# A gated delta rule in a two-block kernel: chunks worked in pairs, and a version with three chunks interleaved

## The chip, the cores and the metric

The kernel runs on one core of a Trainium2 chip, all in fp32. The metric is the time of one execution on the device in microseconds; lower is better. It is a long program of many stages (projections, scans, two attentions, a delta rule, merges), and each stage ends with a barrier of all engines. The change touches one stage, the delta rule, and two tables of constants that it reads.

## What is computed

The stage is the gated delta rule of the second block, run forwards and backwards over 1280 tokens (256 of context, then 1024), for 8 heads of 64 channels, in chunks of 64 tokens, so 20 chunks:

```python
gc = cumsum(g)                                       # per chunk
decay = exp(gc_i - gc_j), lower triangle
lower = strict_lower((k*beta) @ k.T * decay);  A = lower + I
u, w  = solve(A, v*beta), solve(A, k*beta*exp(gc))
qk    = (q @ k.T) * decay
# then, chunk after chunk
v_new = u - w @ S
o     = (q*exp(gc)) @ S + qk @ v_new
S     = S*exp(gc_last) + (k*exp(gc_last-gc)).T @ v_new
```

All but the last three lines is independent from chunk to chunk (the solve). The last three lines carry the state S from chunk to chunk (the advance).

## The kernel before, in words

The class is `Delta` (L1819 to L2166). Partitions 0 to 63 hold the forward chunk and partitions 64 to 127 the backward one, so one chunk step works on 2 directions x 8 heads. The inverse of A is built by doubling: a start from the 2x2 blocks, then `ROUNDS` = 5 rounds. In each round, `ym = -(ct_i x xm)`, then `xm += xt x ym` and `xt += ym x xt`, where `ct_i` is the lower triangle masked to the level of the round. The five masked copies are made by GpSimd (L1916), from `lt`.

TensorE works on 64x64 tiles of its array. `product` (L1932), `to_channels` (L1942) and `with_state` (L1950) each issue 16 small matmuls, one for each head and direction, and `tile_position` says on which quarter of the array each runs. With `src` and `dst` equal (both 0 or both 1) only the two diagonal quarters are used, otherwise all four are. Each fp32 matmul of 64x64 appears in the trace as two weight loads and two matmuls, so that one product is 32 + 32 records.

The order of work is written out by hand. `pairs` (L1870) takes chunks two by two: `weave` alternates the steps of `solve(c)` and `solve(c+1)` on every engine, then `advance(c)` and `advance(c+1)` follow one after the other, and then the next pair starts. Every engine runs its instructions in the order in which they are issued; the engines wait for each other on semaphores. Two sets of buffers and the 8 PSUM banks (4 for each chunk) limit the work to two chunks.

The steps of one chunk in the kernel before:

- SP loads q, k and v (L1889) and the gates beta and g (L1890, L1891), two DMAs of each, before each chunk.
- VectorE spreads the gates (L2055 to L2057) and makes k*beta (L2058). TensorE sums the gates (L1964 to L1967, one product of 512 columns and three narrow ones), and ScalarE takes the exponentials (L2128 to L2131). VectorE scales the queries (`qg`, L2061).
- TensorE transposes k, k*beta, q and qg (L1973, 16 transposes). ScalarE and VectorE copy them out (L2134, L2135, L2064).
- TensorE makes the scores (L1980), VectorE masks and decays them (L2069 to L2072), TensorE turns the first level (L1987, L1992), VectorE starts the inverse (L2077, L2079).
- Five rounds: TensorE (L1938), ScalarE takes `ym` out of PSUM (L2144), TensorE two products, VectorE adds them (L2087, L2090); the last round ends with L2011, L2012 and ScalarE's L2148.
- TensorE makes u and w, ScalarE and VectorE copy them (L2151, L2095).
- The advance: products with the state (L1953), `vn` (L2104), the state's decay (L2109), two more products (L1946, L1938), the state (L2111), the output (L2161, L2114), and two stores on ScalarE's DMA queue (L2164, L2165).

Of the kernel before, what the change touches and what calls it, by code (L numbers as in the profile page):

```python
# [14 lines left out]
P = 128  # L15
# [13 lines left out]
CTX = 256  # L29
# [1789 lines left out]
class Delta(Stage):  # L1819


    N = T2 // 64
    HALVES = (slice(0, 64), slice(64, P))
    ROUNDS = 5

    def __init__(self, k, dn, dg, o_dn):
        super().__init__(k, "delta")
        self.dn, self.dg, self.o_dn = dn, dg, o_dn
        t, sig, N = self.tile, self.event, self.N
        self.ones, self.sums, self.tri, self.sm = t("ones", [P, P]), t("sums", [P, 3, P]), t("tri", [P, 8, 64]), t("sm", [P, 2, 256])  # L1830
        two = lambda name, *shape: [t(f"{name}{s}", [P, *shape]) for s in range(2)]
        self.x, self.gb, self.gm, self.gd, self.dec, self.ex, self.gt = two("x", 1536), two("gb", 16), two("gm", 512), two("gd", 16), two("dec", 512), two("ex", 16), two("gt", 8)
        self.kb, self.vb, self.kbg, self.qg, self.kd = two("kb", 512), two("vb", 512), two("kbg", 512), two("qg", 512), two("kd", 512)
        self.tq, self.tk, self.lt, self.qk, self.ct = two("tq", 4, 3, P), two("tk", 4, P), two("lt", 512), two("qk", 512), two("ct", 6, 512)
        self.xm, self.xt, self.ym, self.um, self.wt, self.vn, self.o = two("xm", 512), two("xt", 512), two("ym", 512), two("um", 512), two("wt", 2, 256), two("vn", 512), two("o", 512)
        self.consts, self.cleared = sig("dma", "consts", 2), sig("dve", "cleared", 1)
        self.loaded = [sig("dma", f"loaded{s}", 6 * N // 2) for s in range(2)]
        self.stored = [sig("dma", f"stored{s}", 2 * N // 2) for s in range(2)]
        (self.gated, self.scaled_q, self.copied_q, self.lowered, self.ct0, self.qk_ready, self.w_copied, self.v_new, self.state, self.outputs) = (
            sig("dve", x, N) for x in ("gated", "scaled_q", "copied_q", "lowered", "ct0", "qk_ready", "w_copied", "v_new", "state", "outputs"))  # L1840
        self.vbeta, self.dec_masked, self.decayed = (sig("pool", x, N) for x in ("vbeta", "dec_masked", "decayed"))
        self.decays, self.copied_k, self.final, self.u_copied, self.o_copied = (sig("act", x, N) for x in ("decays", "copied_k", "final", "u_copied", "o_copied"))
        (self.summed, self.turned, self.scored, self.flipped, self.moved, self.u_made, self.w_made, self.ws, self.qs, self.grown, self.inner) = (
            sig("pe", x, N) for x in ("summed", "turned", "scored", "flipped", "moved", "u_made", "w_made", "ws", "qs", "grown", "inner"))
        R = self.ROUNDS
        self.xt_ready, self.xm_ready, self.levels = sig("dve", "xt_ready", N * R), sig("dve", "xm_ready", N * R), sig("pool", "levels", N * R)
        self.y_made, self.y_copied = sig("pe", "y_made", N * R), sig("act", "y_copied", N * R)
        self.x_fix, self.xt_fix = sig("pe", "x_fix", N * (R - 1)), sig("pe", "xt_fix", N * R)

# [4 lines left out]
    @staticmethod  # L1854
    def heads(t):
        return t.rearrange("p (h b d) -> p b h d", b=2, h=4)

# [4 lines left out]
    def mask(self, l, rows=slice(0, P)):  # L1862
        return bc(self.tri[rows, l].unsqueeze(1), [rows.stop - rows.start, 8, 64])

    @staticmethod
    def turn(c, i, n):

        return 2 * n * (c // 2) + 2 * i + c % 2

    def pairs(self, solve, advance):  # L1870
        for c in range(0, self.N, 2):
            yield from weave(solve(c), solve(c + 1))
            yield from advance(c)
            yield from advance(c + 1)

    def sp(self):
        SP, N = self.nc.sync, self.N
        SP.dma_start(self.sums[:], self.a["c_sums"]).then_inc(*self.consts.inc())
        SP.dma_start(self.tri[:], self.a["c_tri"]).then_inc(*self.consts.inc())
        for c in range(N):  # L1880
            s = c % 2
            x, gb, loaded = self.x[s], self.gb[s], self.loaded[s]
            if c >= 2:
                SP.wait_ge(*self.scaled_q(c - 2))
                SP.wait_ge(*self.decayed(c - 2))
                SP.wait_ge(*self.turned(c - 2))
            for j, first in enumerate((c * 64, CTX + 64 * (N - 1 - c))):
                rows, tokens = self.HALVES[j], slice(first, first + 64)
                SP.dma_start(x[rows], self.dn[tokens, :]).then_inc(*loaded.inc())  # L1889
                SP.dma_start(gb[rows, 0:8], self.dg[tokens, 8 * j:8 * j + 8]).then_inc(*loaded.inc())  # L1890
                SP.dma_start(gb[rows, 8:16], self.dg[tokens, 16 + 8 * j:24 + 8 * j]).then_inc(*loaded.inc())  # L1891
            yield

    def pool(self):
        self.nc.gpsimd.wait_ge(*self.consts(1))
        yield from self.pairs(self.pool_solve, lambda c: iter(()))

    def pool_solve(self, c):
        G, s, h3 = self.nc.gpsimd, c % 2, self.h3
        k_, v_ = self.x[s][:, 512:1024], self.x[s][:, 1024:1536]  # L1900
        beta, ex = self.gb[s][:, 0:8], self.ex[s]
        G.wait_ge(*self.loaded[s](6 * (c // 2) + 5))
        if c >= 2:
            G.wait_ge(*self.outputs(c - 2))
        G.tensor_tensor(h3(self.vb[s][:]), h3(v_), self.per(beta), ALU.mult).then_inc(*self.vbeta.inc())
        yield
        G.wait_ge(*self.decays(c))
        G.tensor_tensor(h3(self.dec[s][:]), h3(self.dec[s][:]), self.mask(0), ALU.mult).then_inc(*self.dec_masked.inc())
        G.wait_ge(*self.gated(c))
        G.tensor_tensor(h3(self.kd[s][:]), h3(k_), self.per(ex[:, 8:16]), ALU.mult)  # L1910
        G.tensor_tensor(h3(self.kbg[s][:]), h3(self.kb[s][:]), self.per(ex[:, 0:8]), ALU.mult).then_inc(*self.decayed.inc())
        yield
        yield
        G.wait_ge(*self.lowered(c))
        for l in range(2, 7):
            G.tensor_tensor(h3(self.ct[s][:, l - 1]), h3(self.lt[s][:]), self.mask(l), ALU.mult).then_inc(*self.levels.inc())  # L1916
        yield

    def pe(self):
        PE = self.nc.tensor  # L1920
        PE.wait_ge(*self.consts(1))
        PE.wait_ge(*self.cleared(0))
        yield from self.pairs(self.pe_solve, self.pe_advance)

    def places(self):

        for j in range(4):
            for par in range(2):
                for r in range(2):
                    yield r, par, j, slice(64 * (2 * j + par), 64 * (2 * j + par) + 64)  # L1930

    def product(self, bank, left, right, src=0, dst=0):  # L1932


        for r, par, j, cols in self.places():
            i, o = r ^ (src & par), r ^ (dst & par)
            rows = self.HALVES[i]
# [544 lines left out]
```

## Time and profile before

| what | value |
|---|---|
| runs of the kernel before | 5002.05 us median of 3 (4998.92 to 5014.29) |
| the profiled execution | 5008.63 us |
| its span in the trace | 5006.8 us |
| TensorE, VectorE, ScalarE, GpSimd busy, whole program | 69%, 47%, 25%, 19% |
| instructions, whole program | 74740, of these 31808 matmuls and 31808 weight loads |

A line of the profile's list of groups gives source line, engine, operation, output and inputs, shapes and count, then busy time and mean duration, then the idle time of the engine just ahead of it and what ended it ("issue" is idle time that nothing in the profile explains). A line of the timeline begins with the start and the duration in us. A group of matmuls in it ends when the last result is out of the array, and the next group can start before that, so the pace of products is read from start to start.

### The profile page before, as it was taken

To read this page: it belongs to the slowest core of one execution; us is meant where nothing else is said; L and a number is where in the kernel's file an instruction comes from. 1 tells how busy PE (TensorE), PEld (TensorE's weight loads), DVE (VectorE), ACT (ScalarE), POOL (GpSimd) and SP (SyncE) were. 2 spreads that over 40 slices of the span, in tenths; PEclk is the share of its full clock that TensorE was granted. 3 is DMA by queue.
4 is the path that set the end of the run, shared out by engine and by line. 5 is a ranking of instruction groups with operands and counts; after the bars stand their busy time and mean duration, and the time that the engine had idled before them with its cause. 6 is when DMAs were issued, how large, how long until landed. Compare 5 with 4: busy or idle time off the path is not lost. (4 is left out here: it accounts for less than half of the span.)

```text
span 5006.8 us, 74740 instructions
## 1 busy us (share of the span) xinstructions
PE 3460.5 (69%) x31808; PEld 2829.7 (57%) x31808; DVE 2352.9 (47%) x3815; ACT 1237.1 (25%) x2052; POOL 951.9 (19%) x761
## 2 busy tenths in 40 slices
PE   4997554664879955547493998971566577777588
PEld 4996443243379954435343997960455466666233
DVE  2113885474621158857564101115578645545333
ACT  2112330243321123314332111101243322222232
POOL 1211332010011123310011112201111133333100
PEclk9997666897989965569795999985677689889789
DMA  3231003432323210031223212213322111110421
GB/s 121 95 101 47 20 20 106 124 82 93 114 91 103 81 41 20 14 112 34 84 98 112 76 63 98 99 62 129 144 96 81 53 27 35 37 35 22 168 82 44
DMA packets 244971, 383.33 MB, mean 77 GB/s; under 512 B 48223, under 2 KB 188439, under 8 KB 243228
## 3 DMA queue, kind: packets, MB, share of 16 engines
q1 hardware_dynamic: 146218, 253.10, 15.8%
q10 hardware_dynamic: 98422, 125.45, 7.3%
q8 instruction: 252, 4.13, 0.3%
q14 instruction: 79, 0.65, 0.0%
HBM read 261.61 MB, written 123.03 MB: 77 GB/s over the span
## 5 line engine op out<-in xcount | busy, mean ns | idle before, releaser
L350 PE MATMUL psum<-proj_w_low,h_high 128*128 128x344 f32 (+1 forms) x2016 | 664.9, 330 | 54.6 <-POOL proj_w_low L334 54.6
L350 PE MATMUL psum<-proj_w_high,h_high 128*128 128x344 f32 (+1 forms) x2016 | 663.2, 329 | 0.0
L350 PE MATMUL psum<-proj_w_high,h_low 128*128 128x344 f32 (+1 forms) x2016 | 663.0, 329 | 0.0
L369 DVE COPY proj_y<-psum 128x344 f32<-128x344 f32 (+1 forms) x126 | 67.8, 538 | 921.7 <-PE psum L350 921.7
L350 PEld LDWEIGHTS psum<-proj_w_low,h_high 128*128 128x128 f32 x2016 | 380.7, 189 | 59.2 <-issue 55.7
L350 PEld LDWEIGHTS psum<-proj_w_high,h_low 128*128 128x128 f32 x2016 | 380.4, 189 | 3.9
L350 PEld LDWEIGHTS psum<-proj_w_high,h_high 128*128 128x128 f32 x2016 | 380.4, 189 | 3.7
L334 POOL TENSOR_TENSOR proj_w_low<-proj_raw,proj_cut 128x2752 fp32r<-128x2752 f32 (+1 forms) x30 | 193.1, 6437 | 976.8 <-DVE proj_cut L363 976.8
L393 ACT ACTIVATE proj_y<-psum 128x344 f32<-128x344 f32 (+1 forms) x126 | 59.2, 470 | 732.8 <-PE psum L350 732.8
L1247 PE MATMUL psum<-merge_wo,merge_yt 128*128 128x512 f32 x512 | 226.7, 601 | 13.4 <-ACT merge_yt L1192 10.0
L950 PE MATMUL psum<-diff_kk,diff_q 64*128 64x512 f32 x512 | 136.3, 653 | 104.8 <-ACT diff_w L1033 71.5
L350 PE MATMUL psum<-proj_latents_w_low,h_high 128*128 128x448 f32 x512 | 189.6, 370 | 20.1 <-POOL proj_latents_w_low L334 20.1
L1033 ACT ACTIVATE diff_w<-psum,diff_nm 128x1024 f32<-128x1024 f32 x128 | 142.5, 1114 | 242.0 <-DVE diff_nm L1003 233.7
L525 PE MATMUL psum<-scan_mqs,scan_mks 64*128 64x128 f32 (+1 forms) x2048 | 162.6, 383 | 46.8 <-DVE scan_am L651 42.8
L350 PE MATMUL psum<-roj_latents_w_high,h_high 128*128 128x448 f32 x512 | 189.3, 370 | 0.0
L350 PE MATMUL psum<-roj_latents_w_high,h_low 128*128 128x448 f32 x512 | 189.3, 370 | 0.0
L1527 PE MATMUL psum<-na_kk,na_q 64*128 64x512 f32 (+2 forms) x320 | 90.4, 719 | 142.3 <-DMA na_v<-proj 102.8
L525 PEld LDWEIGHTS psum<-scan_mqs,scan_mks 64*128 64x128 f32 (+1 forms) x2048 | 144.3, 280 | 66.9 <-issue 58.1
L1247 PEld LDWEIGHTS psum<-merge_wo,merge_yt 128*128 128x128 f32 x512 | 97.3, 193 | 133.8 <-issue 116.7
L651 DVE COPY_PREDICATED scan_am<-scan_lmask,psum 128x512 f32<-128x512 uint32 x224 | 162.5, 725 | 16.5 <-PE psum L525 10.8
L1002 DVE TENSOR_REDUCE diff_nm<-psum 128x1 f32<-128x1024 f32 x128 | 156.3, 1221 | 20.6 <-PE psum L950 20.3
L369 DVE COPY proj_latents_y<-psum 128x448 f32<-128x448 f32 x32 | 20.0, 625 | 295.1 <-PE psum L350 295.1
(418 smaller groups left out, 7300.9 us busy)
## 6 DMA issues: line engine op xcount, KB each, us to landing
proj_raw<-in_w_in SPq DMA_DIRECT2D x24, 1376.0 KB, 6.8
proj<-proj_y ACTq DMA_DIRECT2D x192, 172.0 KB, 1.9
dn_prep_x<-proj SPq DMA_DIRECT2D x24, 768.0 KB, 7.0
delta_x<-dn_qkv SPq DMA_DIRECT2D x40, 384.0 KB, 4.1
proj_latents_raw<-in_w_in SPq DMA_DIRECT2D x8, 1792.0 KB, 7.7
proj<-proj_latents_y ACTq DMA_DIRECT2D x64, 224.0 KB, 1.9
proj<-proj_y ACTq DMA_DIRECT2D x60, 216.0 KB, 1.9
norm_x<-x_stream SPq DMA_DIRECT2D x24, 512.0 KB, 3.2
```

What stands on the lines that cost most here:

```text
L334: G.tensor_tensor(self.wl[:, c % 2], self.raw[:], self.cut[:], ALU.subtract).then_inc(*self.low.inc())
L350: last = PE.matmul(self.ps[:, j % 4, 0:self.width], hp[:, kt, tokens], wp[:, c % 2, kt, :], start=kt == 0 and n == 0, stop=kt == KT - 1 an ...
L369: V.tensor_copy(self.y[:, j % 4, :], self.ps[:, j % 4, 0:self.width]).then_inc(*self.copied[1].inc())
L393: S.activation(self.y[:, j % 4, :], self.ps[:, j % 4, 0:self.width], ACT.Copy).then_inc(*self.copied[0].inc())
L525: last = PE.matmul(out, mk[rows, l, tile, :], mq[rows, l, tile, :], start=True, stop=True, tile_position=(rows.start, 0))
L651: placed = V.copy_predicated(dst, mask.bitcast(U32), sc)
L950: last = PE.matmul(ps[:, 2 * cc + half, :], self.q[rows, s, t * P:(t + 1) * P], self.kk[rows, s, half * 512:(half + 1) * 512], start=True, ...
L1002: c(V.reduce_max(nm[:, z, cc:cc + 1], self.both(cc), axis=AX))
L1033: S.activation(self.w[:, z, cc], self.both(cc), ACT.Exp, bias=self.nm[:, z, cc:cc + 1], scale=0.125, accum_out=self.sm[:, z, cc:cc + 1]).t ...
L1247: last = PE.matmul(ps[:, 4 * s + 2 + half], self.yt[:, s, j * P:(j + 1) * P], self.wo[:, j, half * 512:(half + 1) * 512], start=j == 0, st ...
L1527: last = PE.matmul(ps[:, 2 * h + b, at:at + width], self.q[rows, g, t * P:(t + 1) * P], self.kk[rows, g, c0:c0 + width], start=True, stop= ...
```

## The change

The stage `Delta` is rewritten.

- Three sets of buffers (`SETS = 3`), two PSUM banks for each set and two shared banks for the advance. The order is no longer `pairs` and `weave`: every step of a chunk has a due time written at its `yield` (0 for the first, 20.75 for the last), chunk c starts at 6c (`PACE = 6`), and every engine issues steps in the order of due times, the older chunk first where they are equal. The advance of chunk c-3 (18 to 20.75) so falls among the first steps of chunk c (0 to 2.75).
- The backward direction is mirrored on arrival: two products of TensorE with a reversing matrix, 64 rows by 512 columns each, turn k and v of partitions 64 to 127, and ScalarE writes them back (due 0 and 0.25). The masks are the same for both directions then.
- All gates are loaded once ahead of the first chunk, with four DMAs for each chunk, 80 in all, and TensorE waits for all of them. The loads of q, k, v stay, two DMAs for each chunk.
- A round: the first product uses `lt` itself, not a masked copy; VectorE masks and negates on the way out of PSUM, and only the half of the columns that the level needs; the second product (all four quarters) is as before; the third keeps its two quarters but has 32 moving columns for each matmul, not 64; VectorE adds half of the columns in each of the two sums. ScalarE has no part in the rounds. GpSimd's masked copies are gone.
- The queries are not scaled before the transposes. The product of q and the state is scaled by VectorE when it is copied out. 12 transposes, not 16. `wt` is copied by ScalarE, and `decay` of the state is made by GpSimd, into a second buffer.
- One more narrow product in the gate sums; the mask of the scores with the queries is two VectorE operations of 64 partitions.

The diff, cut to what the text speaks of:

```diff
+    SETS = 3
+    PACE = 6
-    def pairs(self, solve, advance):
-        for c in range(0, self.N, 2):
-            yield from weave(solve(c), solve(c + 1))
-            yield from advance(c)
-            yield from advance(c + 1)
+    def chunks(self, program):
+        return by_time(*(paced(program(c), self.PACE * c, 1) for c in range(self.N)))
...
     def sp(self):
...
+            for rows, t, first in ((self.HALVES[0], at, 0), (self.HALVES[1], back, 8)):
+                SP.dma_start(self.gates[rows, c, 0:8], t[:, first:first + 8]).then_inc(*self.gated_in.inc())
+                SP.dma_start(self.gates[rows, c, 8:16], t[:, 16 + first:24 + first]).then_inc(*self.gated_in.inc())
+        yield from self.chunks(self.sp_chunk)
...
     def pe(self):
+        self.nc.tensor.wait_ge(*self.gated_in(4 * self.N - 1))
...
+        yield 0
+        self.mm(ps[H[1], B, :], 1, 1, self.tri[H[1], 8], x[H[1], 512:1024])
+        self.mm(ps[H[1], B + 1, :], 1, 1, self.tri[H[1], 8], x[H[1], 1024:1536]).then_inc(*self.mirrored.inc())
+        yield 1
...
+            yield 6 + 2 * i
+            for r, par, j in self.places():
+                rows, o = H[r], r ^ par
+                last = self.mm(at(o, col(B + par, 0, j, 64)), r, o, grp(self.lt[s])(rows, par, j), grp(xm)(rows, par, j))
+            last.then_inc(*self.y_made[i].inc())
+            yield 7 + 2 * i
+            PE.wait_ge(*self.y_copied[i](c))
+            if i < R - 1:
+                for r, par, j in self.places():
+                    h, rows = r ^ par, H[r ^ par]
+                    self.mm(at(r, col(B + par, 0, j, 64)), h, r, grp(xt)(rows, par, j), grp(ym[i])(rows, par, j))
+                for r, par, j in self.places():
+                    h, rows = r ^ par, H[r ^ par]
+                    last = self.mm(packed(at(h, col(B, 256 + 128 * par, j, 32)), i), h, h, grp(ym[i])(rows, par, j), side(grp(xt)(rows, par, j), i, 1))
...
+        yield 18
+        for r, par, j in self.places():
+            self.mm(at(r, col(A + par, 256, j, 64)), par, r, tq[H[par], j, 1, H[r]], sm[H[par], r, 64 * j:64 * j + 64])
+        for r, par, j in self.places():
+            last = self.mm(at(r, col(A + par, 0, j, 64)), par, r, wt[H[par], r, 64 * j:64 * j + 64], sm[H[par], r, 64 * j:64 * j + 64])
+        last.then_inc(*self.ws.inc())
+        yield 19
         PE.wait_ge(*self.v_new(c))
         PE.wait_ge(*self.o_copied(c))
...
     def dve_chunk(self, c):
+        yield 0.5
+        V.wait_ge(*self.placed(c))
         V.tensor_copy(gd[0:64, 0:8], g[0:64])
         V.tensor_copy(gd[64:128, 8:16], g[64:128])
         V.tensor_tensor(h3(self.gm[s][:]), self.mask(0), per(g), ALU.mult)
         V.tensor_tensor(h3(self.kb[s][:]), h3(k_), per(beta), ALU.mult).then_inc(*self.gated.inc())
...
+            yield 6.5 + 2 * i
+            V.wait_ge(*self.y_made[i](c))
+            V.tensor_tensor(sides(self.ym[i][s][:], i, 0), part, minus, ALU.mult).then_inc(*self.y_copied[i].inc())
+            yield 7.5 + 2 * i
+            V.wait_ge(*self.fixed[i](c))
+            V.tensor_tensor(left, left, part, ALU.add)
+            V.tensor_tensor(right, right, ps[:, B, 256:512].rearrange("p (b n u) -> p b n u", b=2, u=2 << i), ALU.add).then_inc(*self.updated[i].inc())
+        yield 18.5
         V.wait_ge(*self.ws(c))
...
+        yield 18.75
+        V.tensor_tensor(o, ps[:, A:A + 2, 256:512].rearrange("p b (h d) -> p b h d", h=4), bc(faded.unsqueeze(3), [P, 2, 4, 64]), ALU.mult).then_inc(*self.o_copied.inc())
```

## Rows read from the trace of the kernel before

**Rows 1.** The page: the span, and the queue that carries instructions (packets, MB, share).

```profile
span 5006.8 us, 74740 instructions
...
q8 instruction: 252, 4.13, 0.3%
```

**Rows 2.** Stretches: engines' busy us (instructions), TensorE clock, DMA share, GB/s.

```profile
3975.40:4642.00 666.60, 467.86 (x15840) 420.74 (x15840) 332.32 (x484) 135.01 (x280) 228.50 (x180) 0.89 0.15 36
...
4247.00:4259.00 12.00, 11.00 (x43) 9.25 (x44) 5.79 (x9) 3.10 (x10) 7.36 (x6) 0.57 0.14 38
...
4268.00:4296.00 28.00, 19.63 (x932) 18.53 (x932) 10.99 (x17) 6.35 (x11) 7.01 (x6) 1.00 0.02 5
```

**Rows 3.** Groups of instructions by line in the stage, two that the change removes.

```profile
L1916 POOL TENSOR_TENSOR delta_ct<-delta_lt,delta_tri 128x512 f32<-128x512 f32 x100 | 133.1, 1367 | 19.8 <-DVE delta_lt L2069 19.8
...
L2144 ACT ACTIVATE delta_ym<-psum 128x512 f32<-128x512 f32 x100 | 57.3, 596 | 269.8 <-PE psum L1938 269.8
```

**Rows 4.** The timeline of TensorE: one advance, then within the rounds of a pair.

```profile
4237.64 0.69 PE L1946 MATMUL psum<-delta_vn,delta_kd 64*64 64x64 f32 x32 [0.81 <-ACT delta_o L2161]
...
4239.05 0.97 PE L1938 MATMUL psum<-delta_vn,delta_qk 64*64 64x64 f32 x27 [0.65 <-issue]
...
4270.72 0.68 PE L1938 MATMUL psum<-delta_ym,delta_xt 64*64 64x64 f32 x32
4271.18 1.07 PE L1938 MATMUL psum<-delta_xt,delta_ym 64*64 64x64 f32 x30
4272.04 0.27 PE L1938 MATMUL psum<-delta_ym,delta_xt 64*64 64x64 f32 x2
...
4274.95 0.51 PE L1938 MATMUL psum<-delta_xm,delta_ct 64*64 64x64 f32 x19 [0.58 <-issue]
...
4278.71 0.85 PE L1938 MATMUL psum<-delta_xt,delta_ym 64*64 64x64 f32 x21 [1.08 <-issue]
...
4282.70 0.86 PE L1938 MATMUL psum<-delta_xt,delta_ym 64*64 64x64 f32 x23 [0.98 <-issue]
```

**Rows 5.** The timeline at the stage's start and end, and an earlier row of small DMAs.

```profile
3975.43 0.33 SPq L1878 DMA_DIRECT2D delta_sums<-in_c_sums  x1
...
3982.57 0.60 SPq L1890 DMA_DIRECT2D delta_gb<-dn_gates  x1
3983.21 0.60 SPq L1891 DMA_DIRECT2D delta_gb<-dn_gates  x1
3983.32 0.16 DVE L2055 COPY delta_gd<-delta_gb 64x8 f32<-64x8 f32 x1 [6.67 <-DMA delta_gb<-dn_gates]
...
4639.43 0.34 SPq L2194 DMA_DIRECT2D merge_nw<-in_dn_norm_w  x1
...
L1349 SPq DMA_DIRECT2D rpb_skewed<-rpb_rows x64: 766/767/915, 949.5 to 1000.8; - x64
```

**Rows 6.** Narrow products at the lower clock, and transposes at the higher one.

```profile
4252.47 0.57 PE L1966 MATMUL psum<-delta_gb,delta_sums 128*128 128x8 f32 x2
4252.90 0.59 PE L1967 MATMUL psum<-delta_gd,delta_ones 128*128 128x16 f32 x2
...
3996.92 0.60 PE L1973 MATMUL psum<-ident,delta_x 128*128 128x128 f32 x4
3997.36 0.60 PE L1973 MATMUL psum<-ident,delta_qg 128*128 128x128 f32 x4
```

**Rows 7.** VectorE operations of 256 and of 512 columns, and one beside GpSimd.

```profile
3962.38 0.42 DVE L1752 TENSOR_TENSOR dn_prep_e<-dn_prep_y,dn_prep_rp 128x256 f32<-128x256 f32 x1
...
4265.79 0.67 DVE L2077 TENSOR_TENSOR delta_xm<-delta_tri,psum 128x512 f32<-128x512 f32 x1
...
4245.88 1.46 DVE L2057 TENSOR_TENSOR delta_gm<-delta_tri,delta_gb 128x512 f32<-128x512 f32 x1
```

**Rows 8.** ScalarE: a DMA issue (the first of two), and its next activation.

```profile
4240.90 0.45 ACTq L2164 DMA_DIRECT2D o_dn<-delta_o  x1
...
4242.52 0.60 ACT L2161 ACTIVATE delta_o<-psum 128x512 f32<-128x512 f32 x1 [5.02 <-issue]
```

More of the change, by code:

```diff
@@ L1837, in __init__ @@
[L1837 to L1841, printed above, removed]
@@ L1894, in pool, with sp_chunk @@
+    def sp_chunk(self, c):
+        SP, Z, s = self.nc.sync, self.SETS, c % self.SETS
+        yield -8
+        if c >= Z:
+            SP.wait_ge(*self.gated(c - Z))
+            SP.wait_ge(*self.decayed(c - Z))
+            SP.wait_ge(*self.turned_q(c - Z))
+        for first, rows in zip((c * 64, self.back(c)), self.HALVES):
+            SP.dma_start(self.x[s][rows], self.dn[first:first + 64]).then_inc(*self.loaded[s].inc())
     def pool(self):
         self.nc.gpsimd.wait_ge(*self.consts(1))
-        yield from self.pairs(self.pool_solve, lambda c: iter(()))
@@ L1925, in places @@
[L1925 to L1937, printed above, removed]
-            last = self.nc.tensor.matmul(self.ps[self.HALVES[o], bank + par, 64 * j:64 * j + 64], left[rows, cols], right[rows, cols], start=True, stop=True,
-                                         tile_position=(64 * i, 64 * o))
-        return last
@@ new lines, in pe, with mm @@
+    def pe(self):
+        self.nc.tensor.wait_ge(*self.consts(1))
+        self.nc.tensor.wait_ge(*self.cleared(0))
+        self.nc.tensor.wait_ge(*self.gated_in(4 * self.N - 1))
+        back = self.HALVES[1]
+        self.mm(self.ps[back, 0, 0:16 * self.N], 1, 1, self.tri[back, 8], self.gates[back].rearrange("p c g -> p (c g)")).then_inc(*self.gates_turned.inc())
+        yield from self.chunks(self.pe_chunk)
+    def mm(self, out, i, o, left, right, start=True, stop=True):
+        return self.nc.tensor.matmul(out, left, right, start=start, stop=stop, tile_position=(64 * i, 64 * o))
@@ L2008, in pe_solve @@
-        for r, par, j, cols in self.places():
-            swapped, rows = self.HALVES[r ^ par], self.HALVES[r]
-            out, at = ps[rows, near + par, 64 * j:64 * j + 64], (64 * (r ^ par), 64 * r)
-            PE.matmul(out, eye[swapped], xt[swapped, cols], start=True, stop=False, tile_position=at)
-            last = PE.matmul(out, ym[swapped, cols], xt[swapped, cols], start=False, stop=True, tile_position=at)
-        last.then_inc(*self.xt_fix.inc())
-        yield
-        PE.wait_ge(*self.final(c))
@@ new lines, in pe_chunk @@
+        last.then_inc(*self.grown.inc())
+        yield 20
+        PE.wait_ge(*self.state(c))
+        for r, par, j in self.places():
+            last = self.mm(at(r, col(A + par, 0, j, 64)), r, r, grp(self.qk[s])(H[r], par, j), grp(self.vn[s])(H[r], par, j))
+        last.then_inc(*self.inner.inc())
+    def dve(self):
+        V = self.nc.vector
+        for s in range(self.SETS):
+            V.memset(self.gd[s][:], 0.0)
+            for ym in self.ym:
+                V.memset(ym[s][:], 0.0)
+        V.memset(self.ones[:], 1.0)
```

432 lines of the change are left out of this document (214 added, 218 removed).

## The prediction

> **What bounds the kernel now.** The change touches one stage, so I first took its length. It begins at 3975.4 and the next stage begins at 4639.4 [rows 5], so it is 664.0 us of the profile's 5006.8 [rows 1]. The stretches come second: in 666.6 us TensorE is busy for 468, VectorE for 332, GpSimd for 229, ScalarE for 135 [rows 2]. No engine is full. With first work at 3983.3, ten pairs take 656 us: 65.6 us each, 32.8 for each chunk. The groups by line come third: GpSimd's masked copies (133 us) and ScalarE's evictions in the rounds (57 us, 270 us of waiting ahead of them) lie beside or between TensorE's products [rows 3].
>
> The timeline of the rounds shows what TensorE waits for. A product on four quarters lets the next one start 0.46 us later, one on two quarters 0.86 us later [rows 4]. But at 4274.95, 4278.71 and 4282.70 TensorE stands for 0.58, 1.08 and 0.98 us on "issue", in the middle of a product, 3.76 and 3.99 us apart. Between two such stops lie about 126 matmuls and as many weight loads. The program has 63,616 of these, and the instruction queue brought 252 packets [rows 1], so about 252 instructions each. I read the stops as the arrival of the next packet of TensorE's instructions: **a packet (126 matmuls) takes at least 3.88 us**, however fast the array is. That is an inference from the regular distance. In 28 us of rounds 932 matmuls, 7.4 packets, pass, and 7.4 x 3.88 = 28.7: the rounds are bound by it, at the full clock of 1.00 [rows 2].
>
> **The change, part by part.** In matmul records of one chunk: before, the stage has 15,840 / 20 = 792 [rows 2]. After: mirror 4, sums 10, transposes 12, scores 32, turning 48, rounds 4 x 96 + 32 + 64, u and w 64, advance 128, in sum 778. TensorE's instructions so stay: 778 / 126 = 6.2 packets, a floor of 24.0 us for each chunk.
>
> Start. 80 gate DMAs stand on SP's queue ahead of the first chunk's load, and TensorE waits for the last. Such a DMA takes 0.64 us of the queue (3982.57 to 3983.21), 51.2 us in all. With the loads behind them and 4 us of landing, the first product starts 57.4 us after the stage's begin, where work now starts after 7.9: **+49.5 us**, with no cover, since the stage stands between barriers. Bounds: 0.33 us each, as the first DMA of the stage, gives +25; 0.81 (64 DMAs in 51.3 us, L1349) gives +63 [rows 5].
>
> Prices in the steady state, at the full clock: a product on four quarters 0.46, on two 0.89; results are out 0.23 us after that, and the next engine starts 0.13 later. Mirroring has 4 records of 512 columns on one quarter; 32 records of 64 columns on two quarters take 0.86, so 0.054 each and 1.7 us for mirroring. Four transposes take 0.44 [rows 6]. VectorE takes 0.67 for 512 columns and 0.42 for 256; two SBUF operands beside GpSimd cost 1.46 [rows 7]. ScalarE takes 0.60, so at most 1.2 for the 1024 columns of the mirrored part (I take 1.1); its two DMA issues hold it for up to 1.6, I take 1.3 [rows 8].
>
> The third product of a round, 32 columns on two quarters, has no row. Columns alone would give 0.46. Weight loads may bind instead: narrow products of 8 columns follow each other at 0.43 for two records at the lower clock, 0.11 a record at the full one for 128 weight columns [rows 6], so 0.05 for 64, and on two quarters 0.8. I take 0.75, the row nearest to it. The Trainium skill ("TensorEngine Tiling (Array Packing)", Instruction Overhead) says that a matmul of one column takes as long as one of 60, and to take no factor from a dimension that is already small; by it the product stays at 0.86. Four-quarter records follow at 0.46 / 32 = 14 ns, so no such floor holds across quarters; within one no row decides. By the rule a period would be 0.2 us longer.
>
> One period (6 units of due time) then goes, by the written order, from the start of the mirroring of chunk c:
>
> - mirror 1.9, handoff, ScalarE 1.1, VectorE's gates beside GpSimd's `vb` 2.4, and **only then** `o` of chunk c-3 (due 18.75, behind the gates at 0.5): 0.6. TensorE's next step, `kd` of c-3, waits for that `o`. With handoffs 6.3 us, 4.6 of them idle on TensorE. Three chunks in work do not cover this, since every later product is queued behind `kd`.
> - `kd` 0.46, two double products 2 x 1.21, sums 1.8, ScalarE 1.2, the last of the products issued meanwhile: 6.3 to the transposes.
> - transposes, ScalarE's two copies, then its DMA issues, `final` and the queries' copy: 5.1 to the scores.
> - scores 1.1, VectorE 2.7, turning 1.1, VectorE 1.4, handoffs, `y0` 0.46: 7.2 to the next mirroring.
>
> In sum 24.9 us without the packets. VectorE's work in it is 14, TensorE's 17, GpSimd's 6: none is the bound. The state's own loop (products, `vn`, `kd`, sum) is 4 us and is never last.
>
> Packets. I walked this order with a packet boundary every 128 records (near the 126 read off) and 3.9 us at least between two, from four positions of the boundary in the period. I take it that the idle 4.6 us can't be saved up: at 4239.05 TensorE stops for 0.65 us though it had waited 0.81 shortly before [rows 4]; the dense parts after it stop for 0.6 to 1.9 us three or four times. The periods are 27.9, 28.2, 29.0 and 30.0 us: **28.7**.
>
> Fill and drain: first three periods 22, 23 and 26 us, the last partial ones 20, 13 and 9: 113 us, in place of 3 full periods.
>
> Stage: 57.4 + 113 + 17 x 28.7 = 658.3 us, against 664.0: 5.7 us less. Against the profiled 5008.6 that is 5002.9. That execution is 6.6 us over the median, so I predict **4996 us**. A us in the period is 17 us in the time; that is where the risk lies. What is removed elsewhere (masked copies, ScalarE in the rounds, 4 transposes) I cost at nothing of its own: it is in the order above, and TensorE's packets are the cover.
>
> **The rivals.** About 0.3% (15 us) is what a measurement of this kernel can tell from no change.
>
> A, faster: the packets are fetched further ahead than I think, and the period comes near the written chain, or part of the chain is shorter. For it: the floor of 24.0 us and the chain's 24.9. Against it: the stop shortly after a wait [rows 4]. With 26 us: 57 + 110 + 442 = 609, 55 us less, 4947.
>
> B, slower: the clock. In 4247 to 4259, after an advance in which TensorE mostly waits, the granted clock is 0.57, near the lower level of 1.2 GHz; in the dense rounds it is 1.00 [rows 2]. The change puts an idle stretch of 4.6 us into every period, ahead of a dense part of 6 us. If each is followed by a lower clock, the dense part takes up to 6 us more, about half hidden by the packets: period 31.5, 57 + 118 + 535 = 710, 46 us more, 5048. It decides from about 1.2 us of period on. In its favour the Trainium skill ("TensorE: Matmul & The Clock Gate", HAM oscillation) describes bursts that start cold after each wait, every time; against it, four-quarter products keep the array fuller than the sums and transposes that ran in the slow stretch.
>
> C, slower: VectorE's half-width operations read runs of 2, 4, 8 columns. If one costs as much as a full one, the chain has four more of 0.3: period 30, 22 us over the forecast: 5018.
>
> **Chances.** The forecast (period 27.7 to 29.7) 0.40; A 0.27; B 0.25; C 0.08. The forecast's own range, 4979 to 5013, reaches from faster (a third) to no difference. So faster 0.40, same 0.24, slower 0.36. Its range reaches halfway past A and B, since the start's bounds (-25 and +14) come on top: 4930 to 5065.
>
> **What would show it.** In the profile after: SP issues for 51 us before TensorE's first product of the stage; mirroring starts 28.7 us apart; `kd` waits for `o` with 4 to 5 us of idle TensorE; "issue" stops of about 1 us, 3.9 us apart, in the dense parts; instruction packets unchanged; VectorE's round operations at 0.42; the third product 0.75 from start to start. Wrong would be: gate DMAs far from 0.64 us, products denser than 126 matmuls in 3.9 us, or a granted clock under 0.8 in the steady state (B).

## The result, and the profile after

The change makes the kernel **slower**: 5089.36 us (median of four, 5074.09 to 5102.16) against 5008.17 for the kernel before in the same session. The ratio is 1.0162 [1.0127, 1.0197], so 81 us more. I had forecast 4996, with a range up to 5065.

The profiled execution is the slowest of the four, 5102.16 us. Its page, beside [rows 1], with the busy times:

```profile
span 5100.4 us, 73846 instructions
...
PE 3546.6 (70%) x31530; PEld 2890.3 (57%) x31530; DVE 2313.0 (45%) x3916; ACT 1213.9 (24%) x2013; POOL 829.6 (16%) x681
...
q8 instruction: 249, 4.08, 0.3%
```

The work is what the prediction counted: 278 matmuls fewer (14 for each chunk, less 2 that turn the gates once at the start) and three instruction packets fewer. The engines do less, and still the span is 93.6 us longer.

The stage's own marks say where. First SP's queue and TensorE at the start, then the first and last mirroring copy, and the first DMA of the next stage (timeline, then single lines with minimum, median and maximum duration in ns and the first and last start):

```profile
3973.28 0.33 SPq L1922 DMA_DIRECT2D delta_sums<-in_c_sums  x1
...
L1927 SPq DMA_DIRECT2D delta_gates<-dn_gates x40: 474/596/605, 3974.1 to 4023.9; - x40
...
4031.28 3.67 PE L1984 MATMUL psum<-delta_x,delta_tri 64*64 64x512 f32 x4 [3.42 <-DMA delta_x<-dn_qkv]
...
L2186 ACT ACTIVATE delta_x<-psum x20: 1018/1018/1019, 4035.0 to 4662.5; 64x1024 f32<-64x1024 f32 x20
...
L2248 SPq DMA_DIRECT2D merge_nw<-in_dn_norm_w x1: 336/336/336, 4732.8 to 4732.8; - x1
```

The stage takes 4732.8 - 3973.3 = 759.5 us, where it took 664.0. It divides into five parts:

| part | predicted | measured |
|---|---|---|
| start to the first mirroring | 57.4 | 58.0 |
| first mirroring to its copy | not counted | 3.7 |
| first three intervals between mirroring copies | 22, 23, 26 | 26.3, 25.8, 29.4 |
| the next sixteen | 28.7 each | 34.1 each |
| from the last copy to the end | 70.7 | 70.3 |

The start and the end are as worked out. The stage is 101 us longer than the 658.3 forecast: sixteen periods of 5.4 us too much are 87 of them, the first three intervals 10.5, the first mirroring 3.7. So the question is mostly what lies in a period. Stretches of the kernel after (columns as in [rows 2]): the first interval between mirroring copies, the last of the rounds, the mirroring and the idle stretch in three pieces, the dense part after it, the steady state as a whole, and two single periods out of it:

```profile
4035.00:4061.30 26.30, 15.20 (x155) 10.32 (x158) 6.84 (x12) 3.77 (x9) 4.31 (x4) 0.50 0.19 45
...
4300.00:4317.00 17.00, 15.21 (x594) 14.33 (x592) 8.12 (x17) 3.85 (x7) 4.27 (x4) 0.86 0.26 65
...
4317.00:4321.00 4.00, 1.91 (x17) 0.44 (x6) 1.71 (x5) 1.02 (x1) 0.95 (x1) 1.00 0.02 6
4321.00:4322.00 1.00, 0.00 (x0) 0.00 (x0) 0.99 (x3) 0.00 (x0) 0.09 (x1) 0.89 0.00 0
4322.00:4323.00 1.00, 0.00 (x0) 0.00 (x0) 1.00 (x2) 0.00 (x0) 0.00 (x0) 0.50 0.00 0
...
4323.00:4336.00 13.00, 12.83 (x266) 11.66 (x267) 3.21 (x8) 1.07 (x5) 1.91 (x2) 0.52 0.01 3
...
4152.00:4662.00 510.00, 406.70 (x11671) 356.26 (x11670) 210.91 (x420) 83.44 (x180) 79.71 (x75) 0.78 0.13 31
...
4255.90:4285.30 29.40, 22.29 (x778) 19.63 (x778) 13.85 (x28) 5.54 (x12) 5.33 (x5) 0.94 0.16 39
4489.90:4526.60 36.70, 29.21 (x779) 25.74 (x778) 14.02 (x28) 5.56 (x12) 5.31 (x5) 0.72 0.13 31
```

The granted clock is 1.00 through the mirroring and the first part of the idle stretch, falls shortly before 4322 while TensorE still stands, is 0.50 (the lower level of 1.2 GHz) in the last us of it, and 0.52 in the 13 us after it. The mean of the steady state is 0.78; the kernel before had 0.89 in its stage [rows 2]. By 0.78, some 15 of the 34.1 us of a period run at the lower level (an estimate from these two numbers). The periods differ, and with the clock: with the same 778 or 779 matmuls and about the same wait of `kd`, the one at 0.94 took 29.4 us, near the 28.7 of the forecast, the one at 0.72 took 36.7. Here is the period with the idle stretch above in the timeline:

```profile
4317.03 1.88 PE L1984 MATMUL psum<-delta_x,delta_tri 64*64 64x512 f32 x4
...
4318.95 1.02 ACT L2186 ACTIVATE delta_x<-psum 64x1024 f32<-64x1024 f32 x1 [7.60 <-PE psum L1984]
...
4320.05 1.04 POOL L1957 TENSOR_TENSOR delta_vb<-delta_x,delta_gates 128x512 f32<-128x512 f32 x1 [15.32 <-ACT delta_x L2186]
4320.18 0.94 DVE L2116 COPY delta_gd<-delta_gates 64x8 f32<-64x8 f32 x1
...
4321.74 0.68 DVE L2118 TENSOR_TENSOR delta_kb<-delta_x,delta_gates 128x512 f32<-128x512 f32 x1
4322.34 0.68 DVE L2161 TENSOR_TENSOR delta_o<-psum,delta_ex 128x512 f32<-128x512 f32 x1
4323.17 1.13 PE L1984 MATMUL psum<-delta_vn,delta_kd 64*64 64x64 f32 x32 [4.25 <-DVE delta_o L2161]
4324.05 1.10 PE L1984 MATMUL psum<-delta_ym,delta_xt 64*64 64x64 f32 x32
...
4327.46 1.91 PE L1984 MATMUL psum<-delta_xt,delta_ym 64*64 64x32 f32 x32
...
4329.30 2.07 PE L2003 MATMUL psum<-delta_gm,delta_sums 128*128 128x512 f32 x2
```

`kd` (L1984 in this line: one helper issues all small products) starts 6.14 us after the mirroring and waits 4.25 us for VectorE's `o`, which stands behind the gates of the new chunk. That is the wait that I had forecast, 6.3 and 4.6. What follows is slow: the next product starts 0.88 us after `kd`, where four quarters took 0.46 at the full clock [rows 4]. VectorE's half-width operations are not dear; here is the group that makes `ym`, all rounds, from 4136 to 4663:

```profile
L2144 DVE TENSOR_TENSOR delta_ym<-psum,delta_minus 128x256 f32<-128x256 f32 x78 | 31.9, 422 | 31.0 <-PE psum L1984 28.7
```

### The profile page after: what moved, and what is told of

Its sections match the earlier page's. It is cut to its first block and busy times, and to the rows that moved or that the text cites. A ratio compares the mean times of both kernels' runs of the same rounds, so it can differ in the third digit from the quotient of the medians.

```text
span 5100.4 us, 73846 instructions
## 1 busy us (share of the span) xinstructions
PE 3546.6 (70%) x31530; PEld 2890.3 (57%) x31530; DVE 2313.0 (45%) x3916; ACT 1213.9 (24%) x2013; POOL 829.6 (16%) x681
```

## The experiments

Nine kernels. E1, E2, E6 and E8 change the kernel after in one place; E3, E5 and E7 put E1 and E2 together, E3 and E7 with one more edit; E10 changes the kernel before; E4 is a small kernel by itself. Ratios are to the kernel before on the same chip, with the 95% interval. A ratio below 1 is faster. Periods and clocks are those of the one profiled execution of each kernel, and this is not always the median one: it was 13 us above the median for the kernel after (5102.16), 24 us below it for E2 (4934.54) and 9 us below it for E8 (5015.17), so differences of periods between these come out somewhat too large.

### E1: the gates in 4 DMAs instead of 80

```diff
-        for c in range(N):
-            at, back = self.dg[c * 64:c * 64 + 64], self.dg[self.back(c):self.back(c) + 64]
-            for rows, t, first in ((self.HALVES[0], at, 0), (self.HALVES[1], back, 8)):
-                SP.dma_start(self.gates[rows, c, 0:8], t[:, first:first + 8]).then_inc(*self.gated_in.inc())
-                SP.dma_start(self.gates[rows, c, 8:16], t[:, 16 + first:24 + first]).then_inc(*self.gated_in.inc())
+        ahead = self.dg[0:64 * N].rearrange("(c p) g -> p c g", p=64)
+        back = self.dg[CTX:CTX + 64 * N].rearrange("(c p) g -> p c g", p=64)[:, ::-1]
+        for rows, t, first in ((self.HALVES[0], ahead, 0), (self.HALVES[1], back, 8)):
+            SP.dma_start(self.gates[rows, :, 0:8], t[:, :, first:first + 8]).then_inc(*self.gated_in.inc())
+            SP.dma_start(self.gates[rows, :, 8:16], t[:, :, 16 + first:24 + first]).then_inc(*self.gated_in.inc())
```

> Edit: the 80 gate DMAs of the changed kernel become 4, one for each direction and each of beta and g, with all 20 chunks in each; nothing else. Theory (the start is a plain sum: 80 DMAs of 0.64 us on SP's queue with no cover): the first mirroring moves from 58 us after the stage's begin to 10 to 14 us, and the time falls by 44 to 48 us, from 5089 to about 5043. Rival (descriptors, not issues, are the cost: the 4 DMAs move 5120 pieces of 32 bytes): the first mirroring comes 30 us or more after the begin and the gain is under 30 us. In both the period stays 33 to 34 us.

Measured: 5035.61 us, ratio 1.0075 [1.0053, 1.0096], 0.9% less than the kernel after. One of the two lines of gate DMAs (2 of the 4), and TensorE's first mirroring:

```profile
L1927 SPq DMA_DIRECT2D delta_gates<-dn_gates x2: 663/716/768, 3981.6 to 3984.0; - x2
...
3992.86 3.67 PE L1984 MATMUL psum<-delta_x,delta_tri 64*64 64x512 f32 x4 [1.71 <-DMA delta_x<-dn_qkv]
```

The stage began at 3980.8, so mirroring starts 12.1 us after the begin instead of 58.0. That is 45.9 us less in one place, and by the ratios 0.87%, some 43 us, in the time. The period stays at 33.8 us and the clock at 0.78. The start costs what was predicted and has nothing to do with the miss.

### E2: `o` of the old chunk ahead of the gates of the new one

```diff
     def dve_chunk(self, c):
...
-        yield 0.5
+        yield 0.8
         V.wait_ge(*self.placed(c))
```

The old chunk's `o` is due at 18.75, so 0.75 in the new chunk's count; the gates now come behind it.

> Edit: in the changed kernel VectorE's gates of chunk c get the due time 0.8 in place of 0.5, so the output o of chunk c-3 (0.75) goes ahead of them and the product kd no longer waits for the mirroring, ScalarE's copy and the gates; nothing else. Theory 1 (the idle 4.25 us ahead of kd also lets the clock fall, and the slow stretch of 14 to 17 us after it is what makes the period 34 and not 29): the period falls by more than the idle time, to 27 to 30 us, the granted clock of the steady stretch rises from 0.78 to 0.88 or more, and the time falls by 70 to 110 us. Theory 2 (instruction packets bound the period and the clock only fills time in which TensorE would wait anyway): the period falls by at most 4 us, the clock stays under 0.82, the time falls by 20 to 65 us. Theory 3 (the chain through mirroring, placing, gates and sums is simply moved, since the sums wait for the gates next): the period falls by under 2 us.

Measured: 4959.06 us, ratio 0.9919 [0.9903, 0.9936]. One number in one `yield` takes 2.4%, about 121 us, off the kernel after. The steady state in one stretch, then TensorE around the mirroring of one chunk:

```profile
4120.00:4509.00 389.00, 341.20 (x11987) 302.19 (x11985) 214.09 (x434) 84.34 (x183) 79.95 (x75) 0.94 0.18 43
```

```profile
4305.60 0.35 PE L1984 MATMUL psum<-delta_xm,delta_lt 64*64 64x64 f32 x8 [1.08 <-issue]
4305.77 1.88 PE L1984 MATMUL psum<-delta_x,delta_tri 64*64 64x512 f32 x4
4307.17 0.78 PE L1984 MATMUL psum<-delta_vn,delta_kd 64*64 64x64 f32 x29
```

`kd` follows the mirroring without a wait, the clock is 0.94, and the period is 25.2 us: 8.9 less than 34.1. By the medians it is less, 121 us over the 17 periods with the wait, so 7.1 each. The wait itself was 4.25 us. The rest, 3 to 5 us, came from what followed the wait; E8 shows what that is. The gain is above what either theory expected (70 to 110 us). The stops on "issue" are still there; nothing was done to them.

### E3: mirroring earlier too

E1 and E2 together, and besides:

```diff
     def pe_chunk(self, c):
...
-        yield 0
+        yield -0.25
...
     def act_chunk(self, c):
...
-        yield 0.25
+        yield -0.125
```

> Edit: both edits (4 gate DMAs; o ahead of the gates), and the mirroring gets the due time -0.25 and its copy -0.125, so that it is issued right after the turning of the chunk before, ahead of the products with the state, and runs while VectorE starts the inverse. Theory 1 (idle stretches ahead of dense parts cost the clock): no idle stretch over 2 us is left, granted clock 0.92 or more, period 25 to 27 us, time 4900 to 4945, under the kernel before the change. Theory 2 (packets of 126 matmuls in 3.9 us bound it): the period can't go under 24.0 us and every dense part shows stops; period 26 to 29, time 4925 to 4975.

Measured: 4921.66 us, ratio 0.9845 [0.9827, 0.9863]. The steady state, then two neighbouring stretches of one period:

```profile
4080.00:4489.00 409.00, 354.25 (x11891) 305.95 (x11885) 200.45 (x430) 84.43 (x183) 79.94 (x75) 0.90 0.17 40
...
4316.00:4319.30 3.30, 1.13 (x39) 0.92 (x37) 1.67 (x4) 0.00 (x0) 0.00 (x0) 0.99 0.03 5
4319.30:4326.00 6.70, 6.70 (x130) 4.34 (x130) 1.63 (x4) 1.02 (x1) 0.94 (x1) 0.50 0.01 2
```

The period is 26.6 us and the clock 0.90: not better than the order alone (25.2 and 0.94). The prediction's chain put the mirroring on the path, so an earlier one should have helped, and it didn't. In this trace `kd` again waits for `o`, 1.24 us, but the clock doesn't fall there: in one period only of the twenty is it low as `kd` starts. Nine of the ten falls of the steady state come earlier, within about 3 us of the start of the next mirroring, as in the period shown: TensorE is busy for 1.13 of 3.3 us, and the mirroring, the turning and the products with the state that come next run at 0.50. Why the earlier mirroring brings more of this was not tested.

### E4: streams of TensorE by themselves

A kernel that leaves out all of the reference's work. TensorE runs 20 matmuls of 512 columns on the whole array, then 320 matmuls on four quarters (64 columns), again wide, 320 on two quarters (64 columns), wide, 320 on two quarters with 32 columns, wide:

```diff
+                        PE.matmul(self.ps[H[r ^ par], par, 64 * j:64 * j + 64], self.a[H[r], 64 * j:64 * j + 64], self.b[H[r], 64 * j:64 * j + 64], start=True, stop=True, tile_position=(64 * r, 64 * (r ^ par)))
...
+                        PE.matmul(self.ps[H[h], 2 + par, 64 * j:64 * j + 64], self.a[H[h], 64 * j:64 * j + 64], self.b[H[h], 64 * j:64 * j + 64], start=True, stop=True, tile_position=(64 * h, 64 * h))
...
+                        PE.matmul(self.ps[H[h], 4 + par, 32 * j:32 * j + 32], self.a[H[h], 64 * j:64 * j + 64], self.b[H[h], 64 * j:64 * j + 32], start=True, stop=True, tile_position=(64 * h, 64 * h))
```

> A kernel of its own, which computes nothing of the reference: TensorE alone issues 20 wide matmuls of 512 columns, then 20 products of 16 matmuls on four quarters (64 columns), 20 wide, 20 products on two quarters with 64 columns, 20 wide, 20 products on two quarters with 32 columns, 20 wide. Packet theory (252 instructions take at least 3.88 us, and only one packet is fetched ahead): the four-quarter stream begins at 0.46 us a product and then takes 0.99 a product with stops 3.9 us apart, although 17 us of wide matmuls stood ahead of it; 18 to 20 us in all. Rival (the stops in the large kernel come from something else): 20 x 0.46 = 9.2 us without stops. Half columns: if columns alone count, a product of 32 columns costs 0.46 between stops and the stream is packet-bound at 0.99; if the weight load or a floor of each matmul within its quarter counts, 0.75 to 0.95 between stops and the same as with 64 columns.

Measured (158.15 us for the kernel, one execution; TensorE's timeline):

```profile
17.34 18.89 PE L2437 MATMUL psum<-streams_b,streams_a 128*128 128x512 f32 x40 [17.34 <-DVE streams_a L2432]
36.16 2.90 PE L2446 MATMUL psum<-streams_b,streams_a 64*64 64x64 f32 x182
40.06 2.10 PE L2446 MATMUL psum<-streams_b,streams_a 64*64 64x64 f32 x128 [0.99 <-issue]
43.51 2.10 PE L2446 MATMUL psum<-streams_b,streams_a 64*64 64x64 f32 x128 [1.36 <-issue]
...
69.03 18.88 PE L2455 MATMUL psum<-streams_b,streams_a 64*64 64x64 f32 x640
...
105.21 18.86 PE L2464 MATMUL psum<-streams_b,streams_a 64*64 64x32 f32 x640
```

Two answers. First, the stops: on four quarters TensorE runs exactly 128 matmuls, and 128 weight loads with them, then stands 1.36 us, and does so every 3.45 us. That fits the packet of instructions that the prediction read off [rows 4] (4.13 MB in 252 packets [rows 1], 16.4 KB each), without any other work that could cause it. The pace is faster than expected: 3.45 us and not 3.9, and 15.5 us for the whole stream and not 18 to 20. Only 182 matmul records, 364 instructions with their weight loads, pass before the first stop although 19 us of wide matmuls went ahead, during which the queue had time to fetch: what is left of the packet in work and about one more stand ready, as was taken. Second, the third product: 640 records take 18.88 us at 64 columns and 18.86 at 32, so 0.94 for 32 of them either way. Fewer columns win nothing here. Whether the matmuls or their weight loads set the 0.94 was not separated.

### E5: both repairs

E1 and E2 together, nothing else.

> Edit: the first two experiments together (4 gate DMAs; the gates of VectorE due at 0.8, after o), mirroring left at its due time 0. Theory (the two terms are independent: 0.87% of the time for the start and 2.43% for the order): 0.983 of the kernel before, about 4913 us, period 25.1 us as with the order alone, a little under the version with early mirroring (0.9845, period 26.2). Rival (the early mirroring was worth something that this one lacks): 4930 us or more.

Measured: **4916.69 us, ratio 0.9833 [0.9818, 0.9848]**. The period is 25.6 us.

```profile
4080.00:4470.00 390.00, 336.65 (x11742) 296.89 (x11742) 208.57 (x425) 83.45 (x180) 79.93 (x75) 0.94 0.18 42
```

The two parts add up (86 us below the kernel before; 121 and 43 less than the kernel after, which was 81 above, would make 83). This version beats both kernels.

### E6: the idle stretch filled on one quarter

The kernel after, with the wait left as it is and five needless products of 512 columns issued on one quarter behind the mirroring:

```diff
+        for _ in range(5):
+            self.mm(ps[H[0], B, :], 0, 0, self.tri[H[0], 8], x[H[0], 512:1024])
```

> Edit: the changed kernel as it is, but after the mirroring TensorE issues 5 more products of 64 rows by 512 columns on the quarter (0,0), into PSUM rows that nobody reads (4.3 us, 20 instructions a chunk). The order and the wait for o stay; only the idle stretch of 4.25 us is filled with work that has no use. Theory (the lower clock after the idle stretch, and not the idle time, makes the period 33 us): the granted clock rises from 0.78 to over 0.88, the period falls to 27 to 30 us, which is the walk of the prediction, and the time falls by 50 to 100 us though TensorE does more. Rival (the clock is low because of the sparse products themselves, or one quarter is too little work to count): the clock stays under 0.82 and the time is the same or up to 20 us longer.

Measured: 5069.26 us, ratio 1.0138 [1.0122, 1.0154]. That interval overlaps the one of the kernel after, and 20 us are less than the 50 to 100 of the theory. The period is 32.4 us, 1.7 less, and the clock rises only part of the way (steady state, then `kd` in one period):

```profile
4120.00:4650.00 530.00, 453.39 (x12978) 373.75 (x12976) 228.16 (x456) 92.95 (x202) 89.48 (x84) 0.86 0.14 32
...
4307.47 1.14 PE L1984 MATMUL psum<-delta_vn,delta_kd 64*64 64x64 f32 x32 [1.63 <-DVE delta_o L2163]
```

It separates nothing for certain: the clock came back from 0.78 to 0.86, not to 0.94. And the filling was too short as well as narrow: `kd` still waits 1.63 us in every period, and in the one shown it runs at the lower clock again (1.14 us for its group). Hence E8.

### E7: chunks further apart

E5 with one more edit:

```diff
-    PACE = 6
+    PACE = 8
```

> Edit: the version with both edits, with PACE = 8 in place of 6: a chunk starts 8 due units after the one before, so 2.6 and not 3.5 chunks are in work. Theory (with the wait gone the period is near the floor of the instruction packets, 6.2 x 3.5 to 3.9 = 22 to 24 us, and the overlap of chunks is what brings it there): period 27 to 30 us and the time 35 to 90 us over the version with PACE = 6. Rival (packets bind in both): under 1.5 us of difference in the period, under 30 us in the time.

Measured: 5004.96 us, ratio 1.0012 [0.9998, 1.0025]; 88 us more than E5, all of its gain. The period is 30.3 us, the clock 0.87 in the steady state:

```profile
4120.00:4580.00 460.00, 377.16 (x11913) 327.23 (x11902) 227.28 (x428) 84.70 (x183) 80.91 (x76) 0.87 0.14 35
```

With less of the next chunks' work beside it, TensorE is less full. What E5 gains over the kernel before hangs on the overlap of three and a half chunks; the smaller work of one chunk alone doesn't bring it. Part of the 4.7 us may be the clock's (0.87, not 0.94), and 8 in place of 6 also moves which steps meet on an engine, so this is not a price of overlap by itself.

### E8: the idle stretch filled on all four quarters

The kernel after, its wait untouched; behind the mirroring, 20 needless products of 512 columns, five on each quarter, into banks that chunk c-2 has done with (its `y_copied` is long past):

```diff
+        if c >= 2:
+            PE.wait_ge(*self.y_copied[3](c - 2))
+            flat, free = self.sums[:].rearrange("p a b -> p (a b)"), self.banks(c - 2)
+            for _ in range(5):
+                for r in range(2):
+                    for par in range(2):
+                        self.mm(ps[H[r], free + par, :], r ^ par, r, eye[H[r ^ par]], flat[H[r ^ par]])
```

> Edit: the changed kernel as it is, but after the mirroring TensorE issues 20 products of 64 rows by 512 columns that use all four quarters at once (5 sets of 4, 4.3 us together), into two PSUM banks of chunk c-2 that are empty then; the results are overwritten. Order and waits stay. The filling of one quarter raised the clock from 0.78 to 0.86 only and gave 20 us. Theory (the lower clock after the idle stretch makes the period 33 and not 29): with the whole array busy the granted clock is 0.9 or more, the period 27 to 30 us, the time 50 to 110 us under the changed kernel, 4980 to 5040. Rival (the wait's own time and the packets are the cost, the clock only fills it): clock up, but the period stays over 31 us and the time within 30 us of the changed kernel.

Measured: 5024.38 us, ratio 1.0045 [1.0026, 1.0063]: 1.2%, some 59 us, **less** than the kernel after, for more work. The steady state, then TensorE from the filling on in one period (lines are seven further down in this kernel):

```profile
4140.00:4590.00 450.00, 402.77 (x12496) 320.98 (x12489) 215.32 (x433) 84.50 (x181) 81.01 (x76) 0.97 0.15 35
```

```profile
4318.95 4.82 PE L1984 MATMUL psum<-delta_sums,delta_tri 64*64 64x512 f32 x33
4323.74 0.69 PE L1984 MATMUL psum<-delta_vn,delta_kd 64*64 64x64 f32 x32
4324.23 0.68 PE L1984 MATMUL psum<-delta_ym,delta_xt 64*64 64x64 f32 x32
...
4327.35 0.42 PE L1984 MATMUL psum<-delta_xt,delta_ym 64*64 64x32 f32 x8 [0.37 <-issue]
4327.70 1.13 PE L2010 MATMUL psum<-delta_gm,delta_sums 128*128 128x512 f32 x2
```

`kd` starts no earlier in this period (6.14 us after its first mirroring product), but from it to the sums now pass 3.96 us where the kernel after took 4329.30 - 4323.17 = 6.13. The clock is 0.97 and the period 29.2 us. The order is untouched, the one added wait is long past and the work is more, so the lower clock behind the idle stretch is the cause of what E8 gives back: 4.9 us of period by the two profiles, 3.5 by the medians (59 us over 17 periods). The wait of 4.25 us and these 3.5 are 7.8, near the 7.1 of E2. And 29.2 is near what my walk without the clock gave: 28.7.

### E10: the third product alone, in the kernel before

The kernel before with 32 moving columns in the third product of a round; it leaves out half of each update of `xt`.

```diff
-    def product(self, bank, left, right, src=0, dst=0):
+    def product(self, bank, left, right, src=0, dst=0, n=64):
...
-                self.product(near, ym, xt, src=1, dst=1).then_inc(*self.xt_fix.inc())
+                self.product(near, ym, xt, src=1, dst=1, n=32).then_inc(*self.xt_fix.inc())
```

> Edit: the kernel before the change, with one part of the change alone: the third product of a round (two quarters) has 32 moving columns, not 64. It leaves out half of each update of xt, so this shows a time, not the reference's values. From the streams alone (0.94 us for a product in both widths): no difference, within 10 us of the kernel before. Rival (columns count beside other work): 80 products x 0.4 us, up to 30 us faster.

Measured: 5002.02 us, ratio 1.0000 [0.9988, 1.0011]. In its rounds the stops are where they were:

```profile
4276.37 0.82 PE L1938 MATMUL psum<-delta_xt,delta_ym 64*64 64x32 f32 x21 [0.86 <-issue]
...
4280.33 0.83 PE L1938 MATMUL psum<-delta_xt,delta_ym 64*64 64x32 f32 x23 [0.98 <-issue]
```

3.96 us apart, near the 3.76 and 3.99 of [rows 4]. This part of the change is worth nothing, and the reason is the one that E4 shows.

## Why the prediction was wrong, point by point

**The failed step is the clock.** The sum took the idle stretch at its own 4.6 us and all that follows at the full clock, and so put the clock at nothing: 28.7 us for a period, where 34.1 was measured at a granted clock of 0.78. That is under the 0.8 that the prediction had named as a sign of being wrong. The prediction had it as rival B, with the right place (the idle stretch ahead of `kd`, every period), but with a chance of 0.25 and a price of 46 us over the kernel before. Two arguments held it down, and both fell. First, "four-quarter products keep the array fuller" than the sums and transposes of the slow stretch in the kernel before: the four-quarter `kd` and the product behind it ran at the lower clock all the same, 0.52 over 13 us. Second, "about half hidden by the packets", which gave 31.5 us: of the "up to 6 us" 5.4 came, and the period was 34.1. The slow part behind `kd` was not 6 us long but, in the period shown, about 13, and reached past the sums. From `kd` to the last narrow sum it is 9.1 us there (4323.17 to 4332.30) and 5.5 in E8 (4323.74 to 4329.24); that makes 3.6 of the 4.9 us that E8 brings back. With what the Trainium skill ("TensorE: Matmul & The Clock Gate", HAM oscillation) was cited for, bursts that start cold after each wait, every time, the trace agrees: in all 17 periods in which `kd` waits 4.25 us, the granted clock is at its lower level as `kd` starts or within 0.2 us of it.

I should have read my own rows harder. The stretch at 0.57 in the kernel before stood in [rows 2], and the forecast itself put an idle stretch of that kind into each of 17 periods. With B's period as measured, 34.1, the working of the prediction gives 658.3 + 17 x 5.4 = 750 us for the stage, and 759.5 was measured.

**The fill was mis-sized.** 22, 23 and 26 us were forecast for the first three intervals, 26.3, 25.8 and 29.4 came, 10.5 us more. The first runs wholly at the lower clock (0.50 in the row above, behind 58 us in which TensorE did nearly nothing), and it took 26.3 us in E1, E2, E5 and E8 as well. The first mirroring takes 3.67 us for that reason, and 1.88 later; the sum left out its way to the copy. The clock so has a part in these 10.5 us too; how large a part, no run separates.

**The start was right.** 57.4 us predicted, 58.0 measured. The 40 DMAs of the row, every second one, start from 3974.1 to 4023.9: 49.8 us for 78 steps, 0.64 from one to the next, as priced (0.596, the median of the row, is the duration of one). E1 removes it and gets back about 43 us of the 46 it saves in that place.

**The order of VectorE's steps was right.** 6.3 us from mirroring to `kd` were forecast and 6.14 came; 4.6 of idle time, and 4.25 came. E2 shows what the wait costs with all that hangs on it: 8.9 us of period by the profiles, 7.1 by the medians, for 4.25 of waiting.

**The packets were right.** E4 shows 128 matmuls in 3.45 us, E8 and E2 stops in the rounds too. The 3.88 us of the prediction is the figure under this kernel's own traffic (3.96 in E10); alone it is 3.45. The walk's 28.7 agrees with E8's 29.2, and with the 29.4 of the one period at 0.94 in the kernel after. That it comes so near is in part luck, since two of its terms were wrong in opposite directions (the third product too cheap, ScalarE's DMA issues too dear), and its four periods average 28.8. Rival A in its first form needed packets fetched further ahead, and E4 rules that out. But E2 and E5 reach A's period (25.2 and 25.6) by another way, with the idle stretch gone. Their distance to the floor of 24.0 us is small, and in E2 TensorE's idle time is mostly on "issue", 2.6 of 3.1 us a period; that the packets bind there is read from this, no run supplied instructions faster. That I had not seen: I held the chain of 24.9 plus packets for the limit, where most of the distance to 28.7 was the wait that could be moved for nothing.

**The third product was mis-sized.** I took 0.75 us; 0.94 was measured at 64 and at 32 columns (E4). What I weighed there and left out of the sum agrees with E4: the Trainium skill ("TensorEngine Tiling (Array Packing)", Instruction Overhead) gives no factor for a dimension that is already small. In E4 it holds within one quarter; across quarters its records follow at 2.10 / 128, about 16 ns. The size of the error is small: in E10 the width of the third product makes no difference at all.

**ScalarE's DMA issues were mis-sized.** I had them hold the engine for 1.3 us on the chain. In the kernel after (ScalarE's timeline) they lie beside its activations:

```profile
4304.79 0.60 ACT L2200 ACTIVATE delta_tk<-psum 128x512 f32<-128x512 f32 x1 [4.41 <-PE psum L2012]
4304.80 0.45 ACTq L2219 DMA_DIRECT2D o_dn<-delta_o  x1
4305.29 0.59 ACT L2201 ACTIVATE delta_tq<-psum 128x512 f32<-128x512 f32 x1
4305.29 0.61 ACTq L2220 DMA_DIRECT2D o_dn<-delta_o  x1
4305.95 0.60 ACT L2209 ACTIVATE delta_xt<-psum 128x512 f32<-128x512 f32 x1
```

Activations start 0.50 and 0.66 us apart, and each takes 0.60: at most 0.2 us is lost. It erred towards a longer period, so without it the forecast would have been further off.

**Rival C fell**: 0.422 us for a half-width operation, as priced.

**Left open.** Why the earlier mirroring (E3) gives a lower clock than the order alone. And what share the number of quarters has in E6 and E8: one quarter gave 0.86 and four gave 0.97, but one quarter was also filled for too short a time (1.63 us of waiting left), and nothing between was run.

## What to carry to other kernels

An idle stretch of TensorE ahead of dense work costs more than its length: here 4.25 us of waiting were 7 to 9 us of period, because the work behind it ran at half the clock; price that before calling such a wait small. In an order by due times look at every near tie on every engine, since one `yield` here was worth 2.4% of the whole kernel. A stream of small fp32 matmuls on four quarters was bound by the supply of its instructions (E4), so count instructions and not columns there.

## What the runs showed of the hardware that I had not expected

- The clock fell late in the idle stretch, and the loss came behind it: 1.00 from 4317 to 4321, 0.50 from 4322 on, and still 0.52 from 4323 to 4336, when TensorE was busy for 12.83 of 13 us.
- Needless work made a kernel faster: E8, 59 us, with 20 products more for each chunk.
- 128 matmuls and their weight loads per 3.45 us on four quarters, whatever the array could do; it was done with them in 2.10.
- A copy of 64x8 on VectorE that began while a GpSimd operation was running took 0.94 us (L2116 above): it ended at 4321.12, GpSimd's L1957 at 4321.09. The same copy for the other half (L2115), begun at 4320.00, just ahead of GpSimd's 4320.05, took 0.17.
